# Hybrid mLSTM and attention block on one core: finer first and last adaLN parts, packed gate products, attention's beginning and the last two chunks rearranged

## What is computed

```
mod = silu(c) @ w_ada + b_ada            # 2048 x 12288, six vectors
h = rmsnorm(x, g_norm1) * (1.0 + sc1) + sh1
proj = h @ w_in                          # mq mk mv mo gates(16) aq ak av
m_out = mLSTM(conv(mq, mk), mv, mo, gates)   # 4 heads of 256, both directions
a_out = rmsnorm(windowed_gqa(rope(aq), rope(ak), av, sink))  # 8 heads of 128
x = x + gt1 * (concat(m_out, a_out) @ w_out)
h = rmsnorm(x, g_norm2) * (1.0 + sc2) + sh2
x = x + gt2 * ((silu(h @ w_gate) * (h @ w_up)) @ w_down)
out = rmsnorm(x, g_final)
```

## Time and profile before

| | |
|---|---|
| median of three runs | 2344.12 us (2339.74 to 2346.83) |
| the profiled execution | 2345.41 us, its span on the core 2343.6 us |
| granted PE clock, mean | 0.977 of full |
| busy PE, DVE, ACT, POOL | 97%, 65%, 38%, 10% |

### The profile page before, as it was taken

How to read it: one execution, slowest core, us unless ns; L and a number is a source line. 1 busy time by engine, 2 the same in 40 slices (tenths; PEclk the granted TensorE clock), 3 DMA queues, 4 the chain that set the end, 5 groups by cost and what they waited for, 6 DMA issues and landing times.

```text
span 2343.6 us, 27542 instructions
## 1 busy us (share of the span) xinstructions
PE 2284.2 (97%) x10540; PEld 1894.0 (81%) x10540; DVE 1524.8 (65%) x1732; ACT 888.2 (38%) x1042; POOL 231.5 (10%) x85
## 2 busy tenths in 40 slices
PE   6999999999998999999999999999999999999997
PEld 5878888888876788788888888888888888888886
DVE  5968657474748456667877888788878544444443
ACT  4333232323335312444444444444444433343332
POOL 0002333333320011100000000000000001010100
PEclk7999999999989999999999999999999999999998
DMA  9943444444542368224444444434443855554552
GB/s 361 380 136 122 158 144 145 158 163 145 180 161 73 142 258 310 99 95 139 162 144 150 137 161 145 150 135 161 147 149 133 316 204 188 196 190 180 204 191 108
DMA packets 188194, 405.28 MB, mean 173 GB/s; under 512 B 9280, under 2 KB 67920, under 8 KB 172496
## 3 DMA queue, kind: packets, MB, share of 16 engines
q1 hardware_dynamic: 175088, 388.01, 46.6%
q10 hardware_dynamic: 13024, 16.13, 2.0%
HBM read 384.19 MB, written 19.92 MB: 172 GB/s over the span
## 4 chain that ended last, share of the span: by engine, by line
PE 90%; DVE 4%; issue 2%; DMA 1%; ACT 1%; POOL 1%; SPq 1%; ACTq 0%; POOLq 0%; DVEq 0%
PE ps L1720 27%; PE ps L1721 27%; PE ps L1722 27%; PE ps L1751 1%; PE ps L1870 1%; DMA araw<-in_w_ada 1%; DVE acc L1060 1%; PE ps L2155 1%; DVE acc L1293 1%; PE ps L1883 1%; PE ps L1881 1%; PE ps L1982 1%; PE ps L1770 0%; DVE wlo L1397 0%; PE ps L1859 0%
## 5 line engine op out<-in xcount | busy, mean ns | idle before, releaser
L894 ACT ACTIVATE whi<-wraw 128x1024 fp32r<-128x1024 f32 x200 | 211.0, 1061 | 276.4 <-DVE wraw L1570 153.2
L1551 DVE TENSOR_TENSOR wlo<-wraw,whi 128x1024 fp32r<-128x1024 f32 x200 | 240.5, 1219 | 76.7 <-ACT whi L894 76.7
L1720 PE MATMUL ps<-h_hi,whi 128*128 128x512 f32 x696 | 279.0, 401 | 0.0
L1720 PE MATMUL ps<-d_hi,whi 128*128 128x512 f32 x704 | 274.3, 390 | 0.0
L1722 PE MATMUL ps<-d_hi,wlo 128*128 128x512 f32 x704 | 273.9, 389 | 0.0
L1721 PE MATMUL ps<-d_lo,whi 128*128 128x512 f32 x704 | 273.9, 389 | 0.0
L1722 PE MATMUL ps<-h_hi,wlo 128*128 128x512 f32 x696 | 273.7, 393 | 0.0
L1721 PE MATMUL ps<-h_lo,whi 128*128 128x512 f32 x696 | 273.4, 393 | 0.0
L1661 DVE TENSOR_TENSOR d_lo<-d_raw,d_hi 128x2048 fp32r<-128x2048 f32 x44 | 100.8, 2291 | 244.2 <-ACT d_hi L959 244.2
L1720 PE MATMUL ps<-whi,sk_hi 128*128 128x512 f32 x640 | 250.8, 392 | 0.0
L1722 PE MATMUL ps<-whi,sk_lo 128*128 128x512 f32 x640 | 249.4, 390 | 0.0
(11 more groups left out here) (314 smaller groups left out, 3924.1 us busy)
## 6 DMA issues: line engine op xcount, KB each, us to landing
araw<-in_w_ada SPq DMA_DIRECT2D x64, 1024.0 KB, 5.7
wraw<-in_w_gate SPq DMA_DIRECT2D x88, 512.0 KB, 3.8
wraw<-in_w_up SPq DMA_DIRECT2D x88, 512.0 KB, 4.7
d_raw<-aT_keep SPq DMA_DIRECT2D x44, 1024.0 KB, 4.8
wraw<-in_w_down SPq DMA_DIRECT2D x44, 1024.0 KB, 7.1
wraw<-in_w_in SPq DMA_DIRECT2D x39, 1024.0 KB, 5.3
acc<-in_w_up SPq DMA_DIRECT2D x40, 512.0 KB, 5.4
wraw<-in_w_out SPq DMA_DIRECT2D x16, 1024.0 KB, 8.1
```

The source lines that it names most:

```text
L894: A(EHI[e % 4], src, ACT.Copy).then_inc(uhi_ok, 1)
L1551: V_.tensor_tensor(ELO[e % 4], src, EHI[e % 4].bitcast(F32), ALU.subtract).then_inc(ulo_ok, 1)
L1720: pe.matmul(o, w_hi, m_hi, start=first, stop=False)
```

## The change

**Front.** `PARTS` replaces the quarters: six parts of 2, 2, 4, 4, 2 and 2 tiles. A part of two tiles loads half as many columns (rows of 1 KB in place of 2 KB), and DVE works 14 instructions of 128 x 512 for it. Part p is taken by PE inside the last front slot of part p - 1; `keep_busy` stays ahead of the first front slot alone.

```diff
-        ADA0 = 56
+        PARTS = [(0, 2), (2, 2), (4, 4), (8, 4), (12, 2), (14, 2)]
+        ADA0 = 14 * len(PARTS)
...
-            for n in range(28):
-                quarter, pair = n // 7, n % 7
+                    "p (q c) -> p q c", q=2)[:, :, kt0 * P:(kt0 + nkt) * P]
+
+            for n in range(7 * len(PARTS)):
+                part, pair = n // 7, n % 7
...
-                                 ada_rows(quarter, pair, k)).then_inc(ada_ld[n % 4], 16)
-                if pair in (3, 6):
-                    front_slot(2 * quarter + (pair == 6))
+                    sp.dma_start(RING[(n + RING_0) % 4][:, k * 1024:k * 1024 + 2 * nkt * P].rearrange("p (q c) -> p q c", q=2),
+                                 ada_rows(part, pair, k)).then_inc(ada_ld[(n + RING_0) % 4], 16)
...
+                if pair == 3:
+                    front_slot(kt0 // 2)
+                if pair == 6 and nkt == 4:
+                    front_slot(kt0 // 2 + 1)
```

```diff
-                             (bgate[:], b_gates.rearrange("o g -> g o")),
+                             (wgraw[:], w_in[0, :, COL_G:COL_G + GATES].rearrange("(k p) c -> p k c", p=P)),
                              (posi, positions[0, :].partition_broadcast(P)),
                              (invf[:], rope_inv)):
                 act.dma_start(dst, src).then_inc(const_ld, 16)
+            act.wait_ge(masks_ok, 1)
+            act.dma_start(bgate[0:GATES, :], b_gates.rearrange("o g -> g o")).then_inc(const_ld, 16)
...
+            for j in range(2 * PARTS[0][1]):
                 ada_direct(0, j)
             ada_columns(0)
             keep_busy()
-            for quarter in range(1, 4):
-                front_slot(2 * quarter - 2)
-                front_slot(2 * quarter - 1, quarter)
-                ada_columns(quarter)
-                keep_busy()
-            front_slot(6)
+            def gates_of(part):
+
+                kt0, nkt = PARTS[part]
+                for kt in range(kt0, kt0 + nkt):
+                    pe.matmul(ps[4][0:2 * GATES, :], wg[:, kt, :], h_hi[:, kt, :], start=kt == 0, stop=False)
+                    last = pe.matmul(ps[4][0:2 * GATES, :], wg[:, kt, :], h_lo[:, kt, :], start=False, stop=kt == KT - 1)
+                if kt == KT - 1:
+                    last.then_inc(w_used, 2)
+
+            for part in range(1, len(PARTS)):
+                kt0, nkt = PARTS[part - 1]
+                if nkt == 4:
+                    front_slot(kt0 // 2)
+                front_slot(kt0 // 2 + nkt // 2 - 1, part)
+                ada_columns(part)
+                gates_of(part - 1)
             front_slot(7)
-            pe.wait_ge(wlo_ok, 9)
-            for kt in range(KT):
-                last = mm3(ps[4][:], w3(whi[0], 16)[:, kt, :], w3(wlo[0], 16)[:, kt, :], h_hi[:, kt, :], h_lo[:, kt, :],
-                           kt == 0, kt == KT - 1)
-                if kt in (7, 15):
-                    last.then_inc(w_used, 1)
+            gates_of(len(PARTS) - 1)
```

DVE takes `gates_in` and one half of the convolution ahead of slot 10's low part, the other half and both products behind it:

```diff
             front_lo(9, SLOT)
             gates_in()
+            conv(0, 0)
             front_lo(10, SLOT)
+            conv(0, 1)
+            silu(0, 0)
+            silu(0, 1)
             gate_rows_()
             front_lo(12, SLOT)
             select(0)
```

```diff
-        M_FROM = 6
+        M_AT = [u for u in range(1, 32) if u not in (11, 15, 19, 23, 27)]
+        TWO_BANKS = 12
         EARLY = 4
-        SUM1, SUM2 = KT - 3, KT - 1
+        SUM1, SUM2 = KT - 3, KT - 4
+        WIDE = 4 * NCH - 2
...
-            for i in range(2):
-                evac(qk[:, 2 + i, :], 2 + i, tile_done(5, 1, i))
-            act.wait_ge(w_used, 2 * NB)
...
+            act.wait_ge(w_used, 2 * NB - 2)
+            m_high(0)
+            m_high(1)
+            evac(qk[:, 2, :], 2, tile_done(5, 1, 0))
+            vhi(0, 0, 16)
+            evac(qk[:, 3, :], 3, tile_done(5, 1, 1))
...
-            ROPE_AT = {5: 6, 7: 7, 9: 8, 10: 9}
+            ROPE_AT = {10: 6, 13: 7, 17: 8, 21: 9}
...
 
-                if u in (1, 2):
-                    g = u - 1
-                    dve.wait_ge(mhi_ok, g + 1)
-                    V_.tensor_tensor(o_lo[:, 4 * g:4 * g + 4, :], mT[:, 4 * g:4 * g + 4, :],
-                                     o_hi[:, 4 * g:4 * g + 4, :].bitcast(F32), ALU.subtract).then_inc(mlo_ok, 1)
-                elif u == 3:
+                if u in (3, 5):
+                    i = (u + 9) // 2
+                    ada_b(i % 2, 32, i, 8 + i, False, 16 * (RING_DMAS + 16 + 4))
+                elif u == 8:
                     ada_take(5, 2 + 6, 6)
-                elif u == 4:
-                    dve.wait_ge(modp_ok, 9)
+                elif u == 9:
+                    dve.wait_ge(modp_ok, 5 + len(PARTS))
                     add_bias(2)
                 elif u in ROPE_AT:
                     rope(ROPE_AT[u])
                 elif u in (12, 16, 20, 24):
                     ada_late(u // 4 - 3)
-                elif u in (6, 8):
-                    early_lo(u // 2 - 3)
+                elif u == 11:
...
-                if kind == "end":
-                    pe.wait_ge(modp_ok, 8)
-                    ada_sums(11, 6)
 
```

**End.** Chunks 42 and 43 are made for tokens 0 to 255 first, then for 256 to 511, each half with its own residual, transposes, norm and output:

```diff
+            def turn_half(h):
+                for i in range(4):
+                    pe.wait_ge(d_add, KT + 4 * h + i + 1)
+                    for b in range(2):
+                        tb = 2 * h + b
+                        last = pe.transpose(ps[4 * h + i][:, HT + b * P:HT + (b + 1) * P],
+                                            xr[:, 12 + i, tb * P:(tb + 1) * P], ident[:])
+                    last.then_inc(yt_ps, 1)
+
+            def sum_half(h):
+                pe.wait_ge(y_sb, 12 + 4 * h + 1)
+                pe.wait_ge(sum_ok, h + 2)
+                for b in range(2):
+                    tb = 2 * h + b
+                    last = pe.matmul(ps[4 * h][:, b:b + 1], sqd[:, 0, tb * P:(tb + 1) * P], ones[:, 0:1], start=True, stop=True)
+                last.then_inc(n_ps, 1)
+
+            for h in range(2):
+                part = slice(h * HT, h * HT + HT)
+                for d in (WIDE, WIDE + 1):
+                    pe.wait_ge(dlo_ok, 2 * d + 2 + (h if d > WIDE else 0))
+                    for i in range(4):
+                        if d == WIDE and h == 0:
+                            pe.wait_ge(y_sb, 8 + i + 1)
+                        elif d == WIDE:
+                            pe.wait_ge(d_add, 12 + i + 1)
+                        for k in range(4):
+                            last = mm3(ps[4 * h + i][:, 0:HT], w3(nhi[d % 2], 4)[:, k, i * P:(i + 1) * P],
+                                       w3(nlo[d % 2], 4)[:, k, i * P:(i + 1) * P], d_hi[d % 2][:, k, part],
+                                       d_lo[d % 2][:, k, part], d == WIDE and k == 0, d > WIDE and k == 3)
+                        if d > WIDE:
+                            last.then_inc(d_used, 1)
+                        if h and d == WIDE and i == 1:
+                            turn_half(0)
+                        if h and d == WIDE and i == 3:
+                            sum_half(0)
+            turn_half(1)
+            sum_half(1)
```

More of the change, by code:

```diff
@@ L958, in down_hi @@
                 act.wait_ge(da_ld[d % 2], 16 * (d // 2 + 1))
-                A(d_hi[d % 2][:], d_raw[d % 2][:], ACT.Copy).then_inc(dhi_ok, 1)
+                last = d == 4 * NCH - 1
+                tokens = slice(0, HT if last else S)
+                A(d_hi[d % 2][:, :, tokens], d_raw[d % 2][:, :, tokens], ACT.Copy).then_inc(dhi_ok, 1)
                 act.wait_ge(dw_ld[d % 2], 16 * (d // 2 + 1))
@@ L1745, in x_block, with ada_sums @@
                     last.then_inc(xT_ps, 1)
-            def ada_sums(hidx, bank):
-                pe.wait_ge(ada_acc, hidx * 8 + 8)
-                for j in range(KT):
+            def ada_sums(hidx, bank, part=range(KT)):
+                if part[0] == 0:
+                    pe.wait_ge(ada_acc, hidx * 8 + (ADA0 - 48))
+                for j in part:
                     last = pe.matmul(ps[bank][:, j:j + 1], acc[:, j * P:(j + 1) * P], ones[:, 0:1], start=True, stop=True)
-                last.then_inc(ada_sum, 1)
@@ L1754, in ada_columns @@
-            def ada_columns(quarter):
-                pe.wait_ge(ada_acc, 14 * (quarter + 1))
-                for j in range(8):
-                    c = quarter % 2 * 1024 + j * P
-                    last = pe.matmul(ps[5][:, 8 * quarter + j:8 * quarter + j + 1], acc[:, c:c + P], ones[:, 0:1],
+                if part[-1] == KT - 1:
+                    last.then_inc(ada_sum, 1)
+            def ada_columns(part):
+                kt0, nkt = PARTS[part]
+                pe.wait_ge(ada_acc, 14 * (part + 1))
+                for j in range(2 * nkt):
+                    c = part % 2 * 1024 + j * P
+                    last = pe.matmul(ps[5][:, 2 * kt0 + j:2 * kt0 + j + 1], acc[:, c:c + P], ones[:, 0:1],
@@ L1797, in front_slot @@
                             last.then_inc(w_used, 1)
-                        if then is not None and 2 <= 6 * k + t < 10:
```

(3 more changed lines are left out.)

386 lines of the change are left out of this document (228 added, 158 removed).

## The result

The changed kernel takes 2351.26 us (median of 6 runs, 2350.45 to 2353.57), the kernel before 2343.93 beside it: a ratio of 1.0035, interval 1.0025 to 1.0045, so about 8 us slower (6 to 11). The forecast was 2340, 4 faster. The time lies in the stated range but on the other side of no change.

What follows compares the result with a forecast made beforehand. PE was taken as full nearly everywhere, with PE, DVE and loads all nearly full in the front. Front +2.4, gates' rows +4.1, attention -7.9 and end -3.1 sum to -4.5: 2344.1 becomes 2339.6, say 2340; range 2327 to 2352.

Steps and rivals of the forecast that it cites:

- First modulation, 42.9: Front: first modulation at 42.9 us instead of 48.7, with PE's third x block waiting for constants until 29.
- rival with the constants: Front: slow 64-byte rows hold PE's third x block past 40.5 us; landing at 46 gives 2357; chance 0.10.
- Part 1, 15.7: Front, second part (two tiles): 15.7 us, with 14 DVE accumulations of 0.78 each.
- part 4, 21.0: Front, first narrow part after the wide ones: bound by PE, 21.0 us.
- part 5, 15.7: Front, last narrow part: bound by DVE, 15.7 us.
- Parts 2 and 3, 25.6 each: Front, the two four-tile parts: 25.6 us each, as a quarter before, with the loads at their rate.
- the front's +2.4: Whole front: gates done at 157.3 us against 154.97 before, 2.4 us later.
- From the last modulation to the gates, 10.8: Front's end: h 1.5, front slot 7 8.4 and last gates 0.9, together 10.8 us.
- The gates' rows, +4.1: After the gates: DVE's longer chain brings slot 12's low part later, so PE waits 4.1 us.
- Attention, -7.9: Attention: 7.9 us less, from no `acc` wait, cheaper sums and a clock of 1.00 instead of 0.50.
- End, -3.1: Kernel's end in two halves: 3.1 us less; 256-column matmuls at 0.12 each, 5.6 less after the last matmul.
- The front pays as meant: Rival, chance 0.27: narrow parts fit into DVE's idle time, gates end at 147.5, time 2330.

Runs made afterwards that it cites:

- p0: The changed kernel with the load of the gates' rows last on ACT's queue and on a semaphore of its own, six parts kept: 2342.68 us, ratio 0.9997.
- r2: p1 with each link after the first done as two of 512 columns: 2335.54 us, ratio 0.9970.
- e3: The changed kernel with slot 12's low part on DVE ahead of the copies to the gates' rows: 2346.73 us, ratio 1.0007.
- r3: The changed kernel with 16 one-column products (32 trace records) put back ahead of attention's first scores, result not read: 2355.76 us, ratio 1.0054.
- p1: p0 with four quarters of four tiles instead of six parts: 2328.86 us, ratio 0.9940.
- q3: p1 with SP keeping two pairs of w_ada ahead instead of four, so half the ring: 2359.54 us, ratio 1.0078.

## Why the prediction was wrong

- **First modulation, 42.9: 44.3.** Right in size, by luck, for a wrong reason. I let PE's third x block wait for the constants. It was ACT's issue that stood in the way, 7.55 us at one DMA, ahead of the squares. I had counted the packets of ACT's queue and the PE wait at their end, but not that ACT itself is busy issuing and has the squares behind it. Without the hold and the wait for the landing (p0) it comes at 36.6. My rival with the constants had the right part and the wrong mechanism: it had PE wait past 40 us for them, and the last of their packets was through at about 27.
- **Part 1, 15.7: 16.1; part 4, 21.0: 21.7; part 5, 15.7: 16.1.** Right. A narrow link cost 3.18 / 4 = 0.80 in the chain, where each waits for the one before, and 0.73 on average in r2, where every second one waits. The Trainium skill (VectorE: DVE Perf Modes, The TRN2 errata) has 691 ns measured for an fp32 `tensor_tensor` of 512 elements; the trace agrees for `h_low` within 1% (685 ns), and has 750 for a link of three operands (p0, mean of 8), so most of the 0.80 is the instruction and the rest the wait.
- **Parts 2 and 3, 25.6 each: 28.5 and 26.8. This is the step that failed**, the largest share of what the front's +2.4 was short of the measured +12.2: 4.1 us here, 2.9 behind the last modulation, 1.4 at the first, 1.5 in the other parts. I wrote that "the loads are at their rate; I leave it at 25.6". At their rate they have no slack, so every microsecond that they paused in the narrow parts had to be paid here. I had read the 378 GB/s as one of three full resources. The count of bytes, 10 MB in 26 us, would have told that the loads were the bound of the whole front, and then the question for each edit is only whether SP can go on issuing. It can't where a ring slot is half as large and the engine that frees it pays 0.80 for half the bytes. And the narrow parts' rows of 1 KB moved at 328 to 348 GB/s with the DMA engines full, so these loads were slow even while they ran; the prediction had no term for that.
- **From the last modulation to the gates, 10.8: 13.7.** The forecast took h, front slot 7 and the products at the full clock; PE had idled 1.87 and 1.91 us ahead of it, and the granted clock was 0.69 from 150 to 160 us.
- **The gates' rows, +4.1: a wait of 3.9 at slot 12**, and 0.9 more in that stretch, where the clock is lower behind the wait; I had left that out. e3 shows that the order on DVE makes it.
- **Attention, -7.9: -7.7.** The sum is right. Its part for the clock is supported only so far: the clock did stay at 1.00 from 700 to 730, but with the 32 sums back (r3) it fell for some 3.4 us and not for 17, so the sums alone had not held it down before.
- **End, -3.1: -3.2.** The size is right within what one execution can tell (-5.3 by the median of fifteen). The prediction's "nothing to do" for PE in the last 18.4 us is a misreading, transposes and sums of 2.9 us stand in it, but no term rests on it. 256 columns cost 0.12 each, the row's value:

```profile
2318.20 0.28 PE L1805 MATMUL ps<-d_lo,whi 128*128 128x256 f32 x1
2318.32 0.28 PE L1806 MATMUL ps<-d_hi,wlo 128*128 128x256 f32 x1
```

  The Trainium skill's rule that a weight load overlaps a matmul only where the row groups differ (TensorE: Matmul & The Clock Gate, The mechanism) would by estimate have made it 0.21 (0.107 for the load and as much for the columns); the trace disagrees in this case, at 256 columns as at 512.
- **The rivals.** "The front pays as meant" (0.27) is refuted even without the hold: p0 has `gsb` at 158.3, not 147.5. That number is what quarters with packed gates reach (147.4). The packed gates and their place were worth 7.6 us at that moment (p1); the narrow parts took 10.9 of it back (p0), and the hold and the landing 8.9 more.
- **Range and chances.** What the front was short of was worth 9.8 us on one side, so the range (to 2352) just held it, and slower had 0.17.

## What to carry to other kernels

Ask first whether the loads of a stretch ever pause: if bytes over time is the rate that they reach at best, they are the bound, and an edit is judged by whether the issuing queue can run on. Where the rate is low, look at the share of the DMA engines beside it: a low share is a pause, a full one means that the pieces themselves are dear. I would measure a ring in bytes and not in slots: q3 shows what half the bytes ahead cost, though more slots for smaller pieces were not tried. Smaller pieces also cost the engine that frees them more per byte. A DMA like this one of 2048 small rows is paid by the engine that issues the next DMA and by all that stands behind it there: put it last, with a semaphore of its own (8.9 us here).
